# Folding bias, bonus, weight and gate of y on GpSimd, with the sample tail and the attention entry reordered

## What is computed

```python
y, s_rwkv_new = rwkv7_scan(r4, heads(decay), k4, v4, -kk, kk * a4, s_rwkv.astype(f32))
mean = jnp.mean(y, axis=-1, keepdims=True)
var = jnp.mean((y - mean) ** 2, axis=-1, keepdims=True)
y = ((y - mean) * lax.rsqrt(var + LNX_EPS)).reshape(B, T, RWKV_W) * rwkv_lnx_w + rwkv_lnx_b
bonus = jnp.sum(r4 * k4 * rwkv_r_k, axis=-1, keepdims=True) * v4
y = (y + bonus.reshape(B, T, RWKV_W)) * g
o = jnp.concatenate([o_ret, y], axis=-1).astype(xn.dtype) @ w_out
...
h = x + mix
h = h + memory_attn(rmsnorm(h, g_mem_q), mem_k, mem_v, w_mq, w_mo)
```

## Time and profile before

| | us |
|---|---|
| median of three runs (1854.57 to 1860.58) | 1857.53 |
| the profiled execution | 1854.44 |
| its span, first to last instruction | 1852.6 |

### The profile page before, as it was taken

The page is one execution under the profiler, slowest core; times in us unless marked ns, Lnnn a source line. Parts: engine busy times, 40 slices in busy tenths (PEclk is TensorE's granted clock), DMA queues, the critical chain, the costliest instruction groups (busy, mean ns, idle before and its releaser), DMA issues.

```text
span 1852.6 us, 36222 instructions
## 1 busy us (share of the span) xinstructions
PE 1728.2 (93%) x15104; PEld 1430.1 (77%) x15104; DVE 1176.9 (64%) x1369; ACT 835.1 (45%) x968; POOL 298.5 (16%) x269
## 2 busy tenths in 40 slices
PE   7999999799899987899899999879999999999995
PEld 6999888577777765688688888558888888888882
DVE  5444110589898775524243343479999999999985
ACT  5111221355455424302112112157788787887863
POOL 1332000323232120000000000011121221211105
PEclk9999999799999888999999999979999999999997
DMA  7765416422222128663033232979999999999988
GB/s 285 241 206 188 159 43 210 83 66 69 75 82 69 40 68 308 214 221 116 21 110 96 69 110 111 373 271 401 414 419 413 415 417 412 415 413 416 416 318 301
DMA packets 113271, 420.16 MB, mean 227 GB/s; under 512 B 24244, under 2 KB 42744, under 8 KB 84984
## 3 DMA queue, kind: packets, MB, share of 16 engines
q1 hardware_dynamic: 100888, 374.78, 54.2%
q0 software_dynamic: 7072, 25.69, 3.6%
q10 hardware_dynamic: 5184, 17.82, 2.4%
HBM read 351.27 MB, written 75.36 MB: 230 GB/s over the span
## 4 chain that ended last, share of the span: by engine, by line
PE 51%; DMA 4%; DVE 3%; ACT 2%; issue 2%; SPq 0%; POOL 0%; POOLq 0%; DVEq 0%; ACTq 0%
PE banks L2726 28%; PE banks L2259 5%; PE banks L2263 4%; PE banks L2262 4%; PE banks L2349 2%; PE banks L2337 2%; PE banks L2255 2%; PE banks L2601 1%; DMA at_ring<-w_mv 1%; DMA at_slots<-cache_mem_v 1%; PE banks L2606 1%; PE banks L2360 1%; PE banks L2261 0%; DVE at_x_lo L1789 0%; DMA ex_raw<-w_e_gate 0%
## 5 line engine op out<-in xcount | busy, mean ns | idle before, releaser
L2849 DVE TENSOR_TENSOR ex_wd_lo<-ex_raw,ex_wd_hi 128x2048 fp32r<-128x2048 f32 x62 | 142.0, 2291 | 34.5 <-ACT ex_wd_hi L3025 34.5
L2849 DVE TENSOR_TENSOR ex_wg_lo<-ex_raw,ex_wg_hi 128x2048 fp32r<-128x2048 f32 x66 | 148.4, 2285 | 4.4 <-ACT ex_wg_hi L3025 2.7
L2849 DVE TENSOR_TENSOR ex_wu_lo<-ex_raw,ex_wu_hi 128x2048 fp32r<-128x2048 f32 x64 | 143.5, 2282 | 0.0
L3025 ACT CAST ex_wd_hi<-ex_raw 128x2048 fp32r<-128x2048 f32 x62 | 118.6, 1915 | 44.5 <-PE banks L2726 26.5
L3025 ACT CAST ex_wu_hi<-ex_raw 128x2048 fp32r<-128x2048 f32 x64 | 122.3, 1915 | 30.3 <-PE banks L2726 30.3
L3025 ACT CAST ex_wg_hi<-ex_raw 128x2048 fp32r<-128x2048 f32 x64 | 122.5, 1914 | 10.8 <-DMA ex_raw<-w_e_gate 4.0
L528 PE MATMUL banks<-pj_w_hi,pj_x_hi 128*128 128x448 f32 (+1 forms) x288 | 109.9, 381 | 11.5 <-DVE pj_x_lo L359 11.5
L528 PE MATMUL banks<-pj_w_lo,pj_x_hi 128*128 128x448 f32 (+1 forms) x288 | 109.7, 381 | 0.0
L2726 PE MATMUL banks<-ex_wg_hi,ex_x_hi 128*128 128x512 f32 x256 | 101.0, 395 | 3.5 <-issue 3.0
L2726 PE MATMUL banks<-ex_wu_hi,ex_x_hi 128*128 128x512 f32 x256 | 102.7, 401 | 0.0
L2726 PE MATMUL banks<-ex_wg_hi,ex_x_lo 128*128 128x512 f32 x256 | 100.8, 394 | 0.0
(11 more groups left out here) (505 smaller groups left out, 4375.9 us busy)
## 6 DMA issues: line engine op xcount, KB each, us to landing
ex_raw<-w_e_gate SPq DMA_DIRECT2D x64, 1024.0 KB, 8.0
ex_raw<-w_e_up SPq DMA_DIRECT2D x64, 1024.0 KB, 7.5
ex_raw<-w_e_down SPq DMA_DIRECT2D x64, 1024.0 KB, 7.4
blocks<-ex_y ACTq DMA_DIRECT2D x32, 512.0 KB, 7.7
h<-at_h SPq DMA_DIRECT2D x18, 512.0 KB, 2.6
at_slots<-cache_mem_k SPq DMA_DIRECT2D x8, 1024.0 KB, 11.8
at_slots<-cache_mem_v SPq DMA_DIRECT2D x8, 1024.0 KB, 12.5
pj_w<-w_in SPq DMA_DIRECT2D x8, 896.0 KB, 6.5
```

Of the source, the lines that this page charges most:

```text
L2849: v.tensor_tensor(w_lo(w), raw[:, j], as_f32(w_hi(w)), ALU.subtract).then_inc(S_("w_split"), 1)
L3025: act.copy(w_hi(home(j, n)), raw[:, j]).then_inc(S_("w_high"), 1)
```

## The change

- y of every prompt tile: GpSimd's new `y_fold(i)` makes `tb = (tb + lnx_b) * gate` and `gw = gate * lnx_w` in three steps of 128x512, at the end of its list for a pair; `y_out` on VectorE is then y * root, * gw, + tb. For the sample tile VectorE does the fold itself.
- The sample tail: `products(NT)` doesn't wait for the retention states any more; their products are split and stand behind it. VectorE's list there is rearranged, and all four `Us` copies are ScalarE's. The last rows' stores count on a semaphore of their own, `last_rows`, and the end of the phase doesn't wait for them; the attention does where it reads them.
- The attention's entry: W_V is loaded ahead of the mixed rows; ScalarE copies the keys ahead of W_OUT; on VectorE and ScalarE only the first piece of W_Q stands ahead of `mix_low(0)`. `g_ffn` is loaded during `output` tiles, and the wait for it moves to the first `back_row`.

The diff, cut to its core:

```diff
                 for m in range(HP):
-                    sp.wait_ge(S_("Us_act" if m % 2 == 0 else "Us_dve"), m // 2 + 1)
+                    if m == HP - 1:
+                        sp.wait_ge(S_("U_turned"), 1)
+                        sp.dma_start(d["out_rwkv_p"].rearrange("h v k -> v h k"), heads(yq[0:WN])).then_inc(S_("states_stored"), 16)
+                    sp.wait_ge(S_("Us_copied"), m + 1)
                     sp.dma_start(d["out_rwkv_s"][:, 2 * m:2 * m + 2].rearrange("b p v k -> (p v) b k"), Us[:, m]).then_inc(S_("states_stored"), 16)
-                store_ret(NT)
-                sp.wait_ge(S_("U_turned"), 1)
-                sp.dma_start(d["out_rwkv_p"].rearrange("h v k -> v h k"), heads(yq[0:WN])).then_inc(S_("states_stored"), 16)
-                store_rwkv(NT)
+                sp.wait_ge(S_("o_r_ready"), NT + 1)
+                sp.dma_start(d["mixed"][NT * P:(NT + 1) * P, 0:RW], o_r[:]).then_inc(mx.last_rows, 16)
+                sp.wait_ge(S_("o_w_ready"), NT + 1)
+                sp.dma_start(d["mixed"][NT * P:(NT + 1) * P, RW:D], o_w[:]).then_inc(mx.last_rows, 16)
                 sp.wait_ge(S_("piece_loaded"), 16)
                 sp.wait_ge(S_("states_stored"), 16 * (1 + RP + HP + 1))
-                sp.wait_ge(S_("o_r_stored"), 16 * TILES)
-                sp.wait_ge(S_("o_w_stored"), 16 * TILES)
+                sp.wait_ge(S_("o_r_stored"), 16 * NT)
+                sp.wait_ge(S_("o_w_stored"), 16 * NT)
...
                 def y_out(i):
                     v.wait_ge(S_("y_rn"), i + 1)
                     lk(v.tensor_tensor(heads(y[:]), heads(y[:]), over(sty[:, 4, :], WN), ALU.mult))
-                    lk(v.tensor_tensor(y[:], y[:], V_["rwkv_lnx_w"], ALU.mult))
-                    lk(v.tensor_tensor(y[:], y[:], V_["rwkv_lnx_b"], ALU.add))
-                    lk(v.tensor_tensor(y[:], y[:], tb[:, i % 2], ALU.add))
-                    v.wait_ge(S_("gate_copied"), i + 1)
+                    v.wait_ge(S_("y_folded"), i + 1)
+                    lk(v.tensor_tensor(y[:], y[:], gw[:, i % 3, :], ALU.mult))
                     if i >= 1:
                         v.wait_ge(S_("o_w_stored"), 16 * i)
-                    v.tensor_tensor(o_w[:], y[:], gw[:, i % 3, :], ALU.mult).then_inc(S_("o_w_ready"), 1)
+                    v.tensor_tensor(o_w[:], y[:], tb[:, i % 2], ALU.add).then_inc(S_("o_w_ready"), 1)
...
-                v.wait_ge(S_("bonus"), NT + 1)
-                v.wait_ge(S_("after"), 1)
-                v.tensor_tensor(bk[rows[0]], t0[rows[0]], ex[rows[0], 3], ALU.mult)
-                v.tensor_tensor(bk[rows[1]], kr[rows[1]], ex[rows[1], 3], ALU.mult).then_inc(S_("bk"), 1)
                 turn_evict(NT)
+                roots(NT)
                 for m in range(RP):
                     if m == RP - 1:
                         v.wait_ge(S_("turned"), 4 * NT + 4)
                         for c in range(KC):
                             v.wait_ge(S_("mem_high"), c + 1)
                             v.scalar_tensor_tensor(mem_lo[:, :, c], memT[:, :, c], gkv[:, c:c + 1], mem_hi[:, :, c].bitcast(F32), ALU.mult, ALU.subtract).then_inc(S_("mem_low"), 1)
+                        y_mean(NT - 1)
+                        y_sub(NT - 1)
+                        v.wait_ge(S_("bonus"), NT + 1)
+                        v.wait_ge(S_("after"), 1)
+                        v.tensor_tensor(bk[rows[0]], t0[rows[0]], ex[rows[0], 3], ALU.mult)
+                        v.tensor_tensor(bk[rows[1]], kr[rows[1]], ex[rows[1], 3], ALU.mult).then_inc(S_("bk"), 1)
+                        y_sum(NT - 1)
                     v.wait_ge(S_("Ss_products"), m + 1)
                     v.scalar_tensor_tensor(Ss[:, m].rearrange("p b e -> p (b e)"), Ss[:, m].rearrange("p b e -> p (b e)"), cdec[:, 1, m:m + 1],
                                            PS[:, 6:8, :].rearrange("p a n -> p (a n)"), ALU.mult, ALU.add).then_inc(S_("Ss_ready"), 1)
-                roots(NT)
+                level(NT, 1)
                 masked(NT, 0)
                 masked(NT, 1)
-                y_mean(NT - 1)
-                y_sub(NT - 1)
-                y_sum(NT - 1)
-                level(NT, 1)
                 ret_sum(NT)
+                y_out(NT - 1)
 
                 def spread(h):
                     v.tensor_tensor(bx[:, h], bk[:, hw[h]].unsqueeze(1).to_broadcast([P, DB, WN]), over(seq[:], WN), ALU.mult).then_inc(S_("spread_dve"), 1)
@@ -908,7 +910,6 @@
                 for m in range(HP):
                     ins = v.tensor_tensor(dg[:, m], i64[:].unsqueeze(1).to_broadcast([P, DB, WN]), over(pc[:, 0, m, :], WN), ALU.mult)
                     if m == 1:
-                        y_out(NT - 1)
                         level(NT, 2)
...
-                def state_copy(m):
-                    v.wait_ge(S_("Us_products"), m + 1)
-                    v.tensor_copy(Us[:, m].rearrange("p b k -> p (b k)"), PS[:, m, :]).then_inc(S_("Us_dve"), 1)
-
+                last, gain, shift = slice(0, NS), gw[:, NT % 3, :], tb[:, NT % 2]
+                v.wait_ge(S_("gate_copied"), NT + 1)
+                lk(v.tensor_tensor(shift, shift, V_["rwkv_lnx_b"], ALU.add))
                 y_mean(NT)
                 y_sub(NT)
+                v.tensor_tensor(shift, shift, gain, ALU.mult).then_inc(S_("y_shift"), 1)
+                v.wait_ge(S_("y_shift"), 1)
+                v.tensor_tensor(gain, gain, V_["rwkv_lnx_w"], ALU.mult).then_inc(S_("y_gain"), 1)
+                y_sum(NT)
                 ret_out(NT)
-                y_sum(NT)
-                state_copy(1)
-                y_out(NT)
-                state_copy(3)
+                v.wait_ge(S_("y_rn"), NT + 1)
+                v.wait_ge(S_("y_gain"), 1)
+                lk(v.tensor_tensor(heads(y[:]), heads(y[:]), over(sty[:, 4, :], WN), ALU.mult))
+                lk(v.tensor_tensor(y[:], y[:], gain, ALU.mult))
+                v.wait_ge(S_("o_w_stored"), 16 * NT)
+                v.tensor_tensor(o_w[:], y[:], shift, ALU.add).then_inc(S_("o_w_ready"), 1)
...
+                def y_fold(i):
+                    gain, shift = gw[:, i % 3, :], tb[:, i % 2]
+                    po.wait_ge(S_("gate_copied"), i + 1)
+                    po.wait_ge(S_("tb_ready"), i + 1)
+                    lk(po.tensor_tensor(shift, shift, V_["rwkv_lnx_b"], ALU.add))
+                    lk(po.tensor_tensor(shift, shift, gain, ALU.mult))
+                    po.tensor_tensor(gain, gain, V_["rwkv_lnx_w"], ALU.mult).then_inc(S_("y_folded"), 1)
...
-                for m in (0, 2):
+                for m in range(HP):
                     act.wait_ge(S_("Us_products"), m + 1)
-                    act.copy(Us[:, m].rearrange("p b k -> p (b k)"), PS[:, m, :]).then_inc(S_("Us_act"), 1)
-                act.wait_ge(S_("U_turns"), 1)
-                act.wait_ge(S_("y_sum"), NT + 1)
-                act.copy(yq[0:WN], PS[0:WN, 4, :]).then_inc(S_("U_turned"), 1)
+                    act.copy(Us[:, m].rearrange("p b k -> p (b k)"), PS[:, m, :]).then_inc(S_("Us_copied"), 1)
+                    if m == HP - 2:
+                        act.wait_ge(S_("U_turns"), 1)
+                        act.wait_ge(S_("y_sum"), NT + 1)
+                        act.copy(yq[0:WN], PS[0:WN, 4, :]).then_inc(S_("U_turned"), 1)
...
-                    else:
-                        pe.wait_ge(S_("Ss_ready"), RP)
...
                     if j <= NT:
                         pe.wait_ge(S_("qkT_ready"), j + 1)
                         pe.wait_ge(S_("loraT_ready"), j + 1)
+                    else:
+                        pe.wait_ge(S_("Ss_ready"), RP)
+                        pe.wait_ge(S_("ARK_copied"), 3 * i + 3)
...
                 products(NT)
-                key_products(NT, NT + 1)
+                retention_sample_state(0)
...
+                retention_sample_state(1)
+                level(NT, 1, between=lambda: key_products(NT, NT + 1))
                 AU = lambda m, x: AUs[:].rearrange("p c m t -> p (c m t)")[:, m * P + x * CH:m * P + x * CH + CH]
...
+                    if m == 1:
+                        pe.wait_ge(S_("y_copied"), NT + 1)
+                        pe.wait_ge(S_("U_ready"), 2 * NT)
+                        for n in range(HP):
+                            ins = pe.transpose(PS[0:WN, 4, n * P:(n + 1) * P], U[:, 2 * NT % 3, n, :], ident[:])
+                        ins.then_inc(S_("U_turns"), 1)
...
+                for j in range(NPC):
+                    load_piece(WV, j)
                 load_mixed(0)
                 load_mixed(1)
-                load_x(2)
-                for j in range(NPC):
-                    load_piece(WV, j)
                 for j in range(NPC):
                     load_piece(W_OUT, j)
+                load_x(2)
...
+                    if t == NT - 2:
+                        sp.wait_ge(S_("mix_turned"), NT)
+                        sp.dma_start(gf[:], wide_row(d["g_ffn"][0], D)).then_inc(S_("gf_loaded"), 16)
...
+                    if i == 0:
```

(30 more changed lines are left out.)

36 lines of the change are left out of this document (16 added, 20 removed).

## The result

The changed kernel takes **1871.81 us**, median of five runs (1863.93 to 1873.05), against 1856.29 for the kernel before, its five runs taken together (1851.51 to 1860.58). The ratio is 1.0075, with an interval of 1.0047 to 1.0103: slower by 9 to 19 us. The forecast was 1863.2, slower by 5.7. The range of 1846 to 1874 held the time; the size of the loss was more than twice that of the sum: 13.9 by the ratio.

What follows compares the result with a forecast made beforehand. TensorE was taken to bound the kernel, waiting in each pair for VectorE's state update. Terms 21.9 + 5 - 3.5 - 2.7 - 9.4 - 5.6 = +5.7 us gave a median of 1863.2, range 1846 to 1874.

Steps and rivals of the forecast that it cites:

- What bounds the kernel; y_out covered, operands not: Mixer pairs: TensorE waits for VectorE's state update behind the operands, while y_out's steps lie under 5.7 us of TensorE work.
- Three folds, 1.07 each, +21.9: Mixer pairs: GpSimd's three fold steps delay VectorE by 3.2 us a pair ahead of the state update; +21.9 us in all.
- The clock, +5: Mixer pairs: TensorE's gap lowers its clock in five of seven pairs, at 1.0 us per fall; +5 us.
- The fewer steps of y_out, 0: Pairs 1 to 6: two VectorE steps fewer per tile, all under TensorE's work, gain 0.
- The tail, first part -3.5: Sample tail of the mixers: TensorE's products start without waiting for the retention states; -3.5 us.
- Its end, -2.7: End of the mixers' tail: the phase ends with the fourth state's store, not the last rows' store; -2.7 us.
- The entry, -9.4: Attention's entry: reordered loads, splits and casts let the first output product start earlier at full clock; -9.4 us.
- g_ffn, -5.6: Attention's first query: loading g_ffn earlier removes VectorE's wait and keeps the clock for turn and scores; -5.6 us.
- the ports don't bind: Rival, mixer pairs: GpSimd's folds cost VectorE nothing and the clock doesn't fall; -21.2 us, 1836.3; chance 0.15.
- the entry is bound elsewhere: Rival, attention's entry: W_V and W_OUT pieces, not TensorE, end last, so the 9.4 is lost; +15.1, 1872.6; chance 0.12.
- The clock holds: Rival: TensorE keeps its full clock in the pairs and through the tail; -1.3 us, 1856.2; chance 0.13.

Runs made afterwards that it cites:

- The late fold: Changed kernel with one more wait: GpSimd begins its fold only after VectorE has updated the state of the pair's first chunk; 1837.65 us, ratio 0.9906.
- the kernel without a fold: Changed kernel with the fold of tiles 0 to 7 taken back to VectorE, y_out in five steps; tail, entry and g_ffn stay changed; 1840.15 us, ratio 0.9919.
- the single runs: Kernel before with one part of the change each: fold alone ratio 1.0200, tail alone 0.9984, entry alone 0.9953, g_ffn alone 0.9962.
- the run with the gap filled: Changed kernel with 22 unused transposes (12 in the first pair) on TensorE ahead of the product that waits for the state, pairs 0 to 6; 1857.83 us, ratio 1.0027.

## Why the prediction was right in direction and short in size

- *What bounds the kernel; y_out covered, operands not*: right. The late fold, in y_out's cover, costs nothing that the whole time shows (7 us between the turn copies); the same work ahead of the operands costs 29 us (1.0075 against 0.9919).
- *Three folds, 1.07 each, +21.9*: right. The measured loss is 2.98 in a pair, TensorE's waits in pairs 0 to 6 sum to 19.9, against 21.6. The row of the same shape carried this term. With pair 7, where 0.3 was forecast and TensorE waits 1.2, it is 21.1 against 21.9. With GpSimd's whole length of 1.38 in place of 1.07, as the Trainium skill's "SBUF — State Buffer" has it, the same sum gives 29 (the prediction says 28), and the bounds come to 10 and 34 by their own rows, not 9 and 32; the forecast doesn't hang on either.
- *The clock, +5*: this is the step that failed. The pairs took 281.4 - 248.5 = 32.9 us more than without a fold, 13 beyond the waits, and 12.5 of these stand behind the delayed product. All seven pairs had a stretch at the lower clock, not five, and one is worth 1.8 us, not 1.0; pairs took 38.4 to 41.5 where 37 to 40 was forecast. The price came from pair 4 against pair 3 in before, 36.78 against 35.75; in the kernel without a fold, whose clock is 1.00 in both, they take 36.7 and 35.9. The 1.0 was the pair's own length. The fall cost some 0.5 there (from VectorE's step at 506.47 to the one at 513.21, 6.74 us; 6.27 in the kernel without a fold), although TensorE was 81 to 100% busy: in the doubling levels it takes turns with VectorE and ScalarE. Behind the fold's wait TensorE works through its own list, and everything stretches.
- *The fewer steps of y_out, 0*: nothing shows a gain; with the fold late, three steps instead of five tell no difference.
- *The tail, first part -3.5*: open, likely too large. It was reckoned from rows of an execution whose clock was 0.79 there; at like clocks the new order takes 1 to 4 us less, and the whole time doesn't show it. *Its end, -2.7*: right, 1.7 to 3.3. Together the whole time gives -3 (0.6 to 5) instead of -6.2.
- *The entry, -9.4*: 7.7 in the traces, 8.7 by the ratio. *g_ffn, -5.6*: 6.2 in the traces, 7.0 by the ratio. Both right. (By its own rows the second is 6.2: 3.4 for the start, 1.9 for the scores and 0.9 for the turn, which took 1.94 at the lower clock and takes 1.06.)
- *The rivals*: "the ports don't bind" and "the entry is bound elsewhere" are refuted by the rows and the single runs. "The clock holds" didn't come either; the run with the gap filled shows what it would have given, 1.0027.

So the direction was forecast by a mechanism that the runs bear out, and the size fell short by the clock, 13 for 5, and by the tail, 3 for 6.2. With these the sum is 21.9 + 13 - 3 - 9.4 - 5.6 = +17 against a measured +14 (9 to 19).

## What to carry to other kernels

Work given from VectorE to GpSimd is not free when both read SBUF (a step of two tiles took 0.95 to 1.07 us from VectorE here): find out beside which instructions it will run, and put it, by a wait on the event that ends the critical stretch, beside steps that have a cover. A late operand on TensorE's path is paid twice if the clock falls behind it, so here the gap's length decided. The price of a fall is read where TensorE works through its own list, not where it takes turns with others, busy as it may look there. And the term of a stretch that varies from run to run is not to be read from a single execution: with the entry and g_ffn changed and the fold either left out or begun later, this kernel is 0.8 to 0.9% faster than before, and some 1.6% faster than the change as it was made.

## What was not expected of the hardware

A third of the fold's price can be bought back with useless work: 22 transposes in the gap, none of which makes the state come earlier, are worth 9 us (1.0075 to 1.0027). A gap of 1.1 us in each of six pairs left the granted clock at 1.00 in all six; gaps of 2.0 to 2.2 us took it down in all six. And one step more or less matters in a jump: two waits of 1.1 us in different pairs cost their length, one of 2.2 costs some 1.9 more.
